# Linear attentions with their outputs' tokens on partitions: diagonal score blocks, head norm along the free axis, gates from 512-column products

## What is computed

```
attn = where(lower, q*eb @ (k*enb).T, q*enb @ (k*eb).T)   # GLA, inside one chunk of 64
scores = (q @ k.T) * decay_mat                            # retention, inside one chunk
o = attn @ v + q_fwd @ state_before_this_chunk            # both
o_gla = rms_norm(o_g, gla_norm_g) * silu(gr)              # norm over each head's 64 values
o_ret = rms_norm(o_r, ret_norm_g) * silu(rg)
return concatenate([o_mla, o_gla, o_ret]) @ w_out
```

## Time and profile before

| | |
|---|---|
| median of 3 runs | 2004.95 us (2004.85 to 2008.21) |
| the profiled execution's own time | 2011.03 us |
| its span, first to last instruction | 2008.9 us |
| TensorE busy | 1978.5 us, 98% of the span |
| VectorE, ScalarE, GpSimd (POOL) busy | 749.8, 630.0, 112.3 us |
| mean granted TensorE clock | 0.995 |
| chain that ended last | 96% on TensorE |

### The profile page before, as it was taken

How to read it: one execution, slowest core, us unless ns; L and a number is a source line. 1 busy time by engine, 2 the same in 40 slices (tenths; PEclk the granted TensorE clock), 3 DMA queues, 4 the chain that set the end, 5 groups by cost and what they waited for, 6 DMA issues and landing times.

```text
span 2008.9 us, 23867 instructions
## 1 busy us (share of the span) xinstructions
PE 1978.5 (98%) x10008; PEld 1635.1 (81%) x10008; DVE 749.8 (37%) x879; ACT 630.0 (31%) x864; POOL 112.3 (6%) x172
## 2 busy tenths in 40 slices
PE   7999999999999999999999999999999999999998
PEld 6888888897678888888898888889966788888887
DVE  4333322534555333322442333234354453323313
ACT  4222222324454222321332222233344442322212
POOL 0000000002230000000000000000022300000000
PEclk9999999999999999999999999999999999999999
DMA  4222224221003222223312323332200122222231
GB/s 159 105 95 93 104 85 146 96 100 43 1 22 126 76 92 104 85 104 124 127 45 103 104 84 104 114 138 92 84 22 2 64 99 90 87 101 104 84 115 63
DMA packets 27349, 180.18 MB, mean 90 GB/s; under 512 B 3298, under 2 KB 3460, under 8 KB 7300
## 3 DMA queue, kind: packets, MB, share of 16 engines
q1 hardware_dynamic: 25760, 174.15, 24.2%
q10 hardware_dynamic: 1508, 4.87, 0.8%
HBM read 176.91 MB, written 2.10 MB: 89 GB/s over the span
## 4 chain that ended last, share of the span: by engine, by line
PE 96%; ACT 1%; DVE 1%; issue 1%; POOL 1%; DMA 0%; SPq 0%; POOLq 0%; DVEq 0%; ACTq 0%
PE ps L408 28%; PE ps L410 27%; PE ps L409 27%; PE ps L726 2%; PE ps L619 1%; PE ps L744 1%; PE ps L420 1%; PE ps L540 1%; PE ps L542 1%; PE ps L541 1%; PE ps L733 1%; PE ps L628 1%; PE ps L677 0%; PE ps L671 0%; DMA raw<-stream 0%
## 5 line engine op out<-in xcount | busy, mean ns | idle before, releaser
L408 PE MATMUL ps<-xH,WH 128*128 128x512 f32 (+1 forms) x1728 | 641.9, 371 | 2.8 <-DVE xL L1178 2.8
L410 PE MATMUL ps<-xH,WL 128*128 128x512 f32 (+1 forms) x1728 | 639.4, 370 | 0.0
L409 PE MATMUL ps<-xL,WH 128*128 128x512 f32 (+1 forms) x1728 | 639.3, 370 | 0.0
L1129 DVE TENSOR_TENSOR WL<-raw,WH 128x2048 fp32r<-128x2048 f32 x138 | 316.2, 2291 | 823.4 <-ACT WH L840 811.3
L840 ACT ACTIVATE WH<-raw 128x2048 fp32r<-128x2048 f32 x126 | 241.5, 1917 | 714.1 <-PE ps L410 714.1
L408 PEld LDWEIGHTS ps<-xH,WH 128*128 128x128 f32 x1728 | 326.4, 189 | 58.7 <-issue 4.1
L409 PEld LDWEIGHTS ps<-xL,WH 128*128 128x128 f32 x1728 | 326.2, 189 | 55.6 <-issue 1.0
L410 PEld LDWEIGHTS ps<-xH,WL 128*128 128x128 f32 x1728 | 326.3, 189 | 55.3
L410 PE MATMUL ps<-WH,hL 128*128 128x512 f32 x576 | 224.1, 389 | 0.0
L408 PE MATMUL ps<-WH,hH 128*128 128x512 f32 x576 | 224.1, 389 | 0.0
L409 PE MATMUL ps<-WL,hH 128*128 128x512 f32 x576 | 224.1, 389 | 0.0
(11 more groups left out here) (211 smaller groups left out, 1884.1 us busy)
## 6 DMA issues: line engine op xcount, KB each, us to landing
raw<-stream SPq DMA_DIRECT2D x156, 1024.0 KB, 4.8
norm_g<-norm_gains SPq DMA_DIRECT2D x12, 512.0 KB, 5.4
x<-x_in SPq DMA_DIRECT2D x4, 512.0 KB, 7.9
wq<-w_q_up ACTq DMA_DIRECT2D x4, 512.0 KB
out<-x SPq DMA_DIRECT2D x4, 512.0 KB, 2.6
const<-consts ACTq DMA_DIRECT2D x2, 578.5 KB
wkv<-w_kv_up ACTq DMA_DIRECT2D x2, 512.0 KB
cos<-positions ACTq DMA_DIRECT2D x2, 256.0 KB
```

The source lines that it names most:

```text
L408: mm(dst, wh, xh, start=start, stop=False)
L409: mm(dst, wh, xl, start=False, stop=False)
L410: return mm(dst, wl, xh, start=False, stop=stop)
L1129: tt(wL(slot), raw[:, raw_slot, :], wH(slot).bitcast(F32), ALU.subtract).then_inc(wL_ready, 1)
```

## The change

Input projection: the four slab pairs of values and output gates are arranged anew. `values_pair` (twice) and two calls of `tiles_pair` become four calls of `tokens_pair`, each with 128 tokens stationary and 512 columns of weights moving, over half of the contraction. Gates are now born with tokens on partitions, and ScalarE applies Silu on the way out of PSUM.

Scores: for each chunk its own product (stationary 128\*64, moving 256 columns), chunk 0 to partitions 0 to 63, chunk 1 to 64 to 127. `linear_values`: output with tokens on partitions; stationary is now the chunk's `attn` (64 rows, 64 columns) or its `qx` (128 rows, 64 columns), moving are 64 columns of `v_tok` or of the state. Head norm: squares on ScalarE from PSUM, `reduce_sum` on VectorE, power on POOL for 8 columns a block, all during the steps. `linear_squares` and `linear_spread` fall away; `turn_outputs` (16 transposes, steps 18 to 21) brings the gated outputs back to channels on partitions.

```diff
-                    def values_pair(i, banks):
+                    def tokens_pair(i, banks, second, waits=None, middle=None):
 
                         s = i % 2
                         wait_pair(base + i)
                         for b in range(BLK):
-                            dst = ps[:, banks[b // 2], (b % 2) * GV:(b % 2 + 1) * GV]
-                            for k in range(DT):
-                                at, tok = k * GV, slice(b * P, (b + 1) * P)
-                                mm(dst, xH[:, k, tok], WH[:, s, at:at + GV], start=k == 0, stop=False)
-                                mm(dst, xH[:, k, tok], WL[:, s, at:at + GV], start=False, stop=False)
-                                last = mm(dst, xL[:, k, tok], WH[:, s, at:at + GV], start=False, stop=k == DT - 1)
+                            tok = slice(b * P, (b + 1) * P)
+                            if b == 2:
+                                if waits is not None:
+                                    pe.wait_ge(*waits)
+                                if middle is not None:
+                                    middle()
+                            for n in range(4):
+                                k, cols = 4 * second + n, slice(n * SEQ, (n + 1) * SEQ)
+                                last = three(ps[:, banks[b], :], xH[:, k, tok], xL[:, k, tok], WH[:, s, cols], WL[:, s, cols],
+                                             k == 0, k == DT - 1)
                         last.then_inc(pair_done, 1)
...
-                    values_pair(4, (2, 3))
+                    pe.wait_ge(in_kept, due(in_kept, 6))
+                    tokens_pair(4, (2, 3, 4, 5), False)
...
-                    pe.wait_ge(in_kept, due(in_kept, 6))
-                    values_pair(5, (4, 5))
+                    tokens_pair(5, (2, 3, 4, 5), True)
...
-                    pair(6, (0, 1))
-                    pe.wait_ge(v_kept, due(v_kept, 2))
+                    tokens_pair(6, (0, 1, 2, 3), False, waits=(v_kept, due(v_kept, 1)))
...
-                    pair(7, (2, 3), middle=rotate_rk)
-
-                    pe.wait_ge(in_kept, due(in_kept, 10))
-                    mm(ps[0:QK, 1, :], rot[NOPE:QK, 0:QK], krgg[NOPE:QK, :], start=True, stop=True).then_inc(rot_ready, 1)
+                    tokens_pair(7, (0, 1, 2, 3), True, middle=rotate_rk)
...
-                        mm(ps[:, LIN_BANKS[0], :], kf[:, tok], qx[:, 0, b % 2].rearrange("p h i -> p (h i)"), start=True, stop=True)
-                        mm(ps[:, LIN_BANKS[1], :], kb[:, tok], qx[:, 1, b % 2].rearrange("p h i -> p (h i)"), start=True,
-                           stop=True).then_inc(gated_scored, 1)
+                        for bank, k, kind in ((LIN_BANKS[0], kf, 0), (LIN_BANKS[1], kb, 1)):
+                            for c in range(2):
+                                r = slice(c * CHUNK, (c + 1) * CHUNK)
+                                last = mm(ps[r, bank, 0:GV], k[:, b * P + c * CHUNK:b * P + (c + 1) * CHUNK],
+                                          qx[:, kind, b % 2, :, r], start=True, stop=True)
+                        last.then_inc(gated_scored, 1)
 
                     def retention_scores(b):
-                        tok = slice(b * P, (b + 1) * P)
                         pe.wait_ge(qr_ready, due(qr_ready, b + 1))
                         pe.wait_ge(low_kept, due(low_kept, b + 1))
-                        mm(ps[:, LIN_BANKS[0], :], rk[:, tok], qx[:, 2, b % 2].rearrange("p h i -> p (h i)"), start=True,
-                           stop=True).then_inc(ret_scored, 1)
+                        for c in range(2):
+                            r = slice(c * CHUNK, (c + 1) * CHUNK)
+                            last = mm(ps[r, LIN_BANKS[0], 0:GV], rk[:, b * P + c * CHUNK:b * P + (c + 1) * CHUNK],
+                                      qx[:, 2, b % 2, :, r], start=True, stop=True)
+                        last.then_inc(ret_scored, 1)
 
                     def linear_values(b):
 
                         pe.wait_ge(gr_ready, due(gr_ready, b + 1))
                         for kind, (attn, state) in enumerate(((attn_g, s_gla), (attn_r, s_ret))):
                             for h in range(GH):
-                                rows = slice(DV * (h % 2), DV * (h % 2 + 1))
-                                at = (2 * kind + h // 2) * P
-                                vcol = slice(kind * GV + h * DV, kind * GV + (h + 1) * DV)
-                                last = mm(ps[rows, LIN_BANKS[1], at:at + P], v_tok[:, b, vcol], attn[:, h, :],
-                                          start=True, stop=False)
+                                cols = slice(kind * GV + h * DV, kind * GV + (h + 1) * DV)
                                 for c in range(2):
-                                    n = 2 * b + c
-                                    if n == 0:
-                                        continue
-                                    last = mm(ps[rows, LIN_BANKS[1], at + c * CHUNK:at + (c + 1) * CHUNK],
-                                              state[:, n - 1, h * DV:(h + 1) * DV],
-                                              qx[:, 2 * kind, b % 2, h, c * CHUNK:(c + 1) * CHUNK],
-                                              start=False, stop=c == 1)
+                                    n, r = 2 * b + c, slice(c * CHUNK, (c + 1) * CHUNK)
+                                    last = mm(ps[r, LIN_BANKS[1], cols], attn[r, h, :], v_tok[r, b, cols],
+                                              start=True, stop=n == 0)
+                                    if n:
+                                        last = mm(ps[r, LIN_BANKS[1], cols], qx[:, 2 * kind, b % 2, h, r],
+                                                  state[:, n - 1, h * DV:(h + 1) * DV], start=False, stop=True)
                         last.then_inc(gr_used, 1)
 
-                    def linear_squares(t):
-
-                        pe.wait_ge(o_sq, due(o_sq, t + 1))
-                        for c in range(BLK):
-                            last = mm(ps[:, LIN_BANKS[0], t * 8 + 2 * c:t * 8 + 2 * c + 2], sq[:, t % 2, c * P:(c + 1) * P],
-                                      head_sel, start=True, stop=True)
-                        last.then_inc(o_sq_used if t < 3 else col_ready, 1)
-
-                    def linear_spread(t):
+                    def turn_outputs(t):
 
                         if t == 0:
-                            pe.wait_ge(rstd_ready, due(rstd_ready, 2))
+                            pe.wait_ge(o_gated, due(o_gated, BLK))
                         if t >= 2:
-
-                            pe.wait_ge(o_normed, due(o_normed, t - 1))
-                        for c in range(BLK):
-                            for h in range(2):
-                                at = t * 8 + 2 * c + h
-                                last = mm(ps[h * DV:(h + 1) * DV, LIN_BANKS[t % 2], c * P:(c + 1) * P],
-                                          rstd[:, at:at + 1].broadcast_to([P, DV]), ident[:], start=True, stop=True)
-                        last.then_inc(o_spread if t < 3 else spread_ready, 1)
+                            pe.wait_ge(gatedL_ready, due(gatedL_ready, t - 1))
+                        for b in range(BLK):
+                            last = nc.tensor.transpose(ps[:, LIN_BANKS[t % 2], b * P:(b + 1) * P],
+                                                       o_tok[:, b, t * P:(t + 1) * P], ident[:])
+                        last.then_inc(o_turned, 1)
...
-                        elif NORM_STEP < n <= NORM_STEP + 2:
-                            for t in range(2):
-                                linear_squares(2 * (n - NORM_STEP - 1) + t)
-                        elif GATE_STEP <= n < GATE_STEP + 4:
-                            linear_spread(n - GATE_STEP)
+                        elif TURN_STEP <= n < TURN_STEP + 4:
+                            turn_outputs(n - TURN_STEP)
...
+                    pe.wait_ge(gate_silu, due(gate_silu, 2))
+                    mm(ps[0:QK, 1, :], rot[NOPE:QK, 0:QK], krgg[NOPE:QK, :], start=True, stop=True).then_inc(rot_ready, 1)
                     make_q(0)
 
-                    pe.wait_ge(in_kept, due(in_kept, 12))
+                    pe.wait_ge(gate_silu, due(gate_silu, 4))
                     make_values(0)
...
-                                pe.wait_ge(o_normed, due(o_normed, 4))
+                                pe.wait_ge(gatedL_ready, due(gatedL_ready, 4))
...
-                                up_scores = ps[:, LIN_BANKS[1], :].rearrange("p (h i) -> p h i", h=GH)
-                                for c in range(2):
-                                    r = slice(c * CHUNK, (c + 1) * CHUNK)
-                                    last = af(attn_g[r, :, r], up_scores[r, :, r], ACT.Copy)
-                                last.then_inc(up_kept, 1)
+                                af(attn_g[:], ps[:, LIN_BANKS[1], 0:GV].rearrange("p (h i) -> p h i", h=GH),
+                                   ACT.Copy).then_inc(up_kept, 1)
...
```

(78 more changed lines are left out.)

123 lines of the change are left out of this document (40 added, 83 removed).

## The result

The changed kernel took 2061.02 us (median of 4 runs, 2059.73 to 2062.77) against 2006.58 us of the kernel before on the same chip (2004.85 to 2010.25): ratio 1.0272, 95% interval 1.0259 to 1.0285. It is 54.4 us slower; the forecast was 53.6 us slower.

What follows compares the result with a forecast made beforehand. TensorE was taken to set the time. Terms summed to +8.6 us without the clock, plus 45 us for clock falls in `linear_values`; from the 2004.95 us median this gave 2058.5 us, 2.7% slower, range 2008 to 2085.

Steps and rivals of the forecast that it cites:

- projection, start of the middle: Input projection with 512-column products, -2.4 us, and start of the middle, -1.4 us, over two layers.
- scores with the waits ahead of them: Gated and retention scores as halves beside each other, -7.8 us, and shorter waits ahead, -2 us, over two layers.
- `linear_values` at full clock: Inner and state products in turn, each phase paying a shape change: 28.1 us a layer, +38.2 us for two.
- squares and their falls: Head squares' products go, -7.9 us, and the low clock behind them, 5.1 us: -13.0 us.
- spreads to transposes: Head norm spreads of 4.3 us a layer become 16 transposes of 1.8 us: -5.0 us.
- waits of the light steps: Steps without their linear piece become shorter than the latent attention's round through three engines: +2 us for two layers.
- clock in and behind `linear_values`: Clock falls to half level in the blocks and stays down after: +7 us per long block, +1.5 per short, +45.
- changes of shape: On TensorE, each change of a tile's rows or columns costs 0.09 us, with nothing running beside it.
- The phase: In `linear_values`, the stretch from one shape change to the next: 0.25 us; prediction wrong above all if under 0.21.
- The first rival: 64\*64 and 128\*64 count as one arrangement in `linear_values`, +4.6 us, no clock fall: 1980 us, chance 0.13.
- +1 a layer for waits that appear: Steps that lose their linear piece wait for the latent attention's round: +1 us a layer, +2 in all.
- The late output chain: Rival: last block's `o_gated` comes late, so TensorE waits ahead of `turn_outputs`; each us late is 1 us a layer.

Runs made afterwards that it cites:

- experiment 1: Changed kernel with the inner product of `linear_values` contracted over all 128 rows, zeros in the other chunk's rows: 1997.61 us, ratio 0.9948.
- experiment 4: Kernel before with the head squares' matmuls cut to one product of 8 columns instead of four of 2 (head sums left out): 2001.15 us, ratio 0.9963.
- control of experiment 5: Kernel before with VectorE's row maxima (`tops`) ahead of the linear piece from the step after the linear pieces on: 2007.87 us, ratio 1.0013.
- experiment 2: Changed kernel with both inner products of each head first, then both state products, 16 phases a block, not 32: 2011.83 us, ratio 1.0026.
- experiment 3: Changed kernel with the gated kind's half of each `linear_values` block one step earlier, behind the retention scores: 2036.24 us, ratio 1.0145.

## Why the prediction was right, and where it was off

Each term as forecast, and as the trace of the changed kernel (span 49.4 us longer than that of the profiled execution before) and the experiments give it, both layers, us:

| term | forecast | measured | from |
|---|---|---|---|
| projection, start of the middle | -3.8 | -2.8 | stages |
| scores with the waits ahead of them | -9.8 | -8.3 | pieces of experiment 1's kernel, at full clock: 10.7 to 6.6 a layer |
| `linear_values` at full clock | +38.2 | +39.5 | 16 and 3 x 32 phases: 4.2 and 3 x 8.2 = 28.8 a layer |
| squares and their falls | -13.0 | -12.5 | 7.4 gone, and half of the 10.2 low in the profiled execution |
| spreads to transposes | -5.0 | -5.4 | 4.5 to 1.8 a layer |
| waits of the light steps | +2 | +7.6 | `probT` rows |
| clock in and behind `linear_values` | +45 | about +31 | remainder; bounds below |
| sum | +53.6 | +49.4 | |

The 5.1 us of low level in the squares' term belong to these two executions. Experiment 4 and the control of experiment 5 show that the falls behind the squares can be absent, and the forecast counted them as a gain in the median too, where part of them may never have stood. Spans and medians differ for a related reason: the profiled execution before took 2011.03 us at a granted clock of 0.995, 4.5 above its median of 2006.58, the changed kernel's was at its median.

**Right: changes of shape.** The phase was forecast at 0.25 us and is 0.257, though no row of before showed 64\*64 beside 128\*64. The row on L639, where rows alone differ, carried it. Experiments 1 and 2 show the cause: a pair of products takes 0.117 us where the shape stays, and half the changes take half the time. The first rival (shapes don't part, a phase under 0.21 us) is out. The Trainium skill, TensorEngine Tiling (Array Packing), Key Properties, says that a change of tiling mode drains TensorE; these runs agree, at 0.146 us for a change with the first weights after it, and though the output columns are the same 64.

**Right in kind, too large: the clock.** That the level would fall inside the long blocks and outlast them was forecast, and it did so in all six. Experiment 3 shows it to be a cost of its own: as many changes, 24.8 us less. The size was off in three places. The forecast took some 14 us of low level for each long block; measured are 74.7 / 6 = 12.5. It took 3 us for two short blocks; neither fell. And it took half of low time as lost, but a phase goes from 0.257 to 0.403 us and loses 0.146 of 0.403: by the columns alone it would be 0.107 more, and the change of shape with the first weights adds only some 0.04. Inside the blocks the loss is 35.7 + 35.2 - 2 x 28.8 = 13.3 us; behind them lie 38 us of low level, of which at most half, 19, is lost: 32 at most, 31 as what is left of the sum, which is no measurement of its own. In experiment 3, 24.8 us for 61 us of low level give the same share, 0.41.

The Trainium skill, TensorE: Matmul & The Clock Gate, Why this matters for your kernels, puts drops down to idle gaps between bursts. Here the trace differs: TensorE is busy for 5.10 of 5.10 us ahead of the fall at 578.0 and for 13.70 of 13.70 behind it, and for 6.10 of 6.10 ahead of the one at 557.6. By that page alone the term is 0, and the changed kernel would have stood at about 2030.

**Off: the waits.** "+1 a layer for waits that appear" was 3.8. The forecast named the reason (steps become shorter than the attention's own round) but did not look at what the new output chain puts into VectorE's queue ahead of `tops`. In the changed kernel slow blocks seem to hide part of the wait for `probT`: it is 11.8 us there, 14.4 in experiment 2 with shorter blocks, and 17.4 in experiment 1, 13.2 more than before. That is 11 of the 17.6 us by which experiment 1 (1997.6) missed the first rival's sum (1980), which had +2 for waits. The late output chain ahead of `turn_outputs` did not appear: those pieces start without a wait.

The good agreement of the total is part luck: the clock term was 14 us too high, waits and scores together 7 too low, projection and `linear_values` 2 too low, and the other 5 us are the difference between the profiled spans (49.4) and the medians (54.4).

## What to carry to other kernels

Count the changes of tile shape between neighbouring small matmuls before counting their work: here each cost 0.146 us, more than the 0.107 of a whole 64-column product, so padding 64 rows with zeros to the neighbour's 128 was worth 63 us, and grouping products of one shape 49, both with the low clock that went with it. If a stretch of narrow products must stay, break it up with dense work: in experiment 3 that took away five of six falls of the clock. When work leaves a step that hides another engine's round, ask which queue now carries that round and what stands ahead of it.

## What the hardware showed unasked

The low level does not slow everything by two: a phase with a change of shape in it went from 0.257 to 0.403 us. Two products in different halves of the output partitions run beside each other at 64 columns too: 0.117 us for a pair, where one alone has 0.107 to stream. And the clock's falls differ from one execution to the next: 17 executions of the kernel before on one chip had mean granted clocks from 0.994 to 0.998. The fall in the projection lasted 3.4 us at 433 us and 6.8 at 446 in experiment 4, which has the same projection. The changed kernel had one in its second layer as well (1448 to 1452 us, granted clock 0.57); in the second layer of experiments 1 to 3, with its projection, there was none. What decides it stays open.
